# Start addresses of matmul operands moved apart modulo 512 bytes, in a three-block transformer kernel

## The reference

```python
def swiglu(h, w_in, w_out):
    gate, up = jnp.split(h @ w_in, 2, axis=-1)
    return (jax.nn.silu(gate) * up) @ w_out

def first_block(x, ...):
    h = rms_norm(x, ln_pre_mix[l])
    proj = h @ w_in[l]
    ...
    attn_out = dilated_attention(q, k, v).reshape(B, S, ATTN_WIDTH)
    mix = jnp.concatenate([pool_out, attn_out], axis=-1) @ w_out[l]
    x = x + rms_norm(mix, ln_post_mix[l])
    h = rms_norm(x, ln_pre_ffn[l])
    f = (jax.nn.silu(h @ w_gate[l]) * (h @ w_up[l])) @ w_down[l]
    x = x + rms_norm(f, ln_post_ffn[l])

def second_block(x, ...):
    for i in range(DEPTH_2):
        h = rms_norm_2(x, mix_norm[i])
        j = i // N_MIXERS
        if i % N_MIXERS == 0:
            x = x + retention(h, ret_w_in[j], ret_out_norm[j], ret_w_o[j])
        else:
            x = x + stick_breaking(h, sb_w_in[j], sb_q_norm[j], sb_k_norm[j], sb_w_o[j])
        x = x + swiglu(rms_norm_2(x, ffn_norm[i]), ffn_w_in[i], ffn_w_out[i])
```

## The kernel before

| tensor | before | after |
|---|---|---|
| X, HH | 128 | 128 |
| HL | 128 | 160 |
| WH[0], WH[1] | 128, 128 | 224, 288 |
| WL[0], WL[1] | 128, 128 | 128, 160 |
| RAW[0], RAW[1], ACC, ACCH, ACCL | 128 | 160 |
| MEANR, MEAN, IDENT | 0 | 32 |
| MH, M1H, M2H, M3H | 128 | 224 |
| ML | 128 | 32 |
| M1L / M2L / M3L | 128 | 320 / 384 / 448 |
| G1, SG, U1, HD, F (feed-forward work) | 128 | 32 |

## Time and profile before

### The profile page before, as it was taken

One profiled execution on the slowest core, in us unless ns is written; L12 is line 12 of the kernel. 1 busy time (PEld: TensorE's weight loads), 2 busy tenths in 40 slices (PEclk: granted clock), 3 DMA queues, 4 the chain that ended last, 5 costly groups with the idle time before them and its releaser, 6 DMA issues.

```text
span 1964.0 us, 25749 instructions
## 1 busy us (share of the span) xinstructions
PE 1957.2 (100%) x8959; PEld 1590.7 (81%) x8959; DVE 865.8 (44%) x1148; ACT 801.4 (41%) x1078; POOL 764.9 (39%) x307
## 2 busy tenths in 40 slices
PE   9999999999999999999999999999999999999999
PEld 6777888888888778787888888888777788888887
DVE  5775653433145335333243434224788763433200
ACT  6665533233243433324332223225888752323211
POOL 4223344444413334243444444443222244444443
PEclk9999999999999999999999999999999999999999
DMA  5212122223223222222232223222111122222332
GB/s 172 75 65 86 65 97 96 96 96 115 91 74 123 70 86 91 69 87 85 86 105 98 96 96 102 99 99 85 54 63 46 63 97 96 96 96 96 110 97 93
DMA packets 49013, 177.39 MB, mean 90 GB/s; under 512 B 5569, under 2 KB 6465, under 8 KB 48961
## 3 DMA queue, kind: packets, MB, share of 16 engines
q1 hardware_dynamic: 46656, 172.95, 26.3%
q10 hardware_dynamic: 2304, 3.74, 0.6%
HBM read 174.57 MB, written 2.10 MB: 90 GB/s over the span
## 4 chain that ended last, share of the span: by engine, by line
PE 98%; DVE 1%; ACT 0%; DMA 0%; issue 0%; SPq 0%; DVEq 0%; ACTq 0%
PE B L355 26%; PE B L356 26%; PE B L364 26%; PE B L1114 2%; PE B L1251 2%; PE B L1072 1%; PE B L1076 1%; PE B L1073 1%; PE B L381 1%; PE B L377 1%; PE B L376 1%; PE B L1240 1%; PE B L1296 1%; PE B L1158 1%; PE B L900 1%; PE B L931 1%
## 5 line engine op out<-in xcount | busy, mean ns | idle before, releaser
L595 POOL TENSOR_TENSOR WL<-RAW,WH 128x1024 fp32r<-128x1024 f32 (+1 forms) x296 | 753.9, 2549 | 1171.5 <-PE B L364 763.8
L355 PE MATMUL B<-HH,WH 128*128 128x512 f32 x1608 | 629.1, 391 | 0.3 <-DVE QT L2153 0.3
L356 PE MATMUL B<-HL,WH 128*128 128x512 f32 x1608 | 626.1, 389 | 0.0
L336 ACT CAST WH<-RAW 128x1024 fp32r<-128x1024 f32 (+1 forms) x300 | 329.1, 1098 | 555.6 <-PE B L356 475.0
L364 PE MATMUL B<-HH,WL 128*128 128x512 f32 x1608 | 398.3, 390 | 0.0
L355 PEld LDWEIGHTS B<-HH,WH 128*128 128x128 f32 x1608 | 301.8, 188 | 64.9 <-issue 1.7
L364 PEld LDWEIGHTS B<-HH,WL 128*128 128x128 f32 x1608 | 301.4, 188 | 63.2 <-POOL WL L595 0.4
L356 PEld LDWEIGHTS B<-HL,WH 128*128 128x128 f32 x1608 | 301.9, 188 | 62.4
L1921 DVE TENSOR_TENSOR U<-B,RB 128x512 f32<-128x512 f32 x66 | 45.6, 691 | 294.3 <-PE B L364 294.3
L355 PE MATMUL B<-MH,WH 128*128 128x512 f32 x440 | 171.2, 389 | 0.0
L356 PE MATMUL B<-ML,WH 128*128 128x512 f32 x440 | 171.2, 389 | 0.0
(11 more groups left out here) (377 smaller groups left out, 2257.9 us busy)
## 6 DMA issues: line engine op xcount, KB each, us to landing
RAW<-in_w_small SPq DMA_DIRECT2D x254, 512.0 KB, 3.3
RAW<-in_w_large SPq DMA_DIRECT2D x48, 704.0 KB, 4.1
out_t<-X SPq DMA_DIRECT2D x7, 256.0 KB, 5.2
X<-in_x_t ACTq DMA_DIRECT2D x4, 256.0 KB, 6.2
X<-in_x_t SPq DMA_DIRECT2D x4, 256.0 KB, 6.5
DECAY<-in_decay ACTq DMA_DIRECT2D x4, 256.0 KB, 2.6
RAW<-in_w_small ACTq DMA_DIRECT2D x2, 256.0 KB, 6.5
RAW<-in_w_small SPq DMA_DIRECT2D x2, 256.0 KB, 7.4
```

Source lines behind the costliest of these rows:

```text
L336: act.copy(wh, raw).then_inc(s_hi, 1)
L355: pe.matmul(bank, wh[:, c, :], xh[:, k0 + c, :], start=(start and c == 0), stop=False)
L356: mm = pe.matmul(bank, wh[:, c, :], xl[:, k0 + c, :], start=False, stop=False)
L595: pool.tensor_tensor(wl, raw, wh.bitcast(F32), ALU.subtract).then_inc(s_lo, 1)
```

## The change

No instruction is added, removed or moved on any engine, and no DMA: each engine's list of operations, operands, shapes and counts is the same, only source line numbers differ. What changes is where tensors lie. Unused tensors (`PHASE_HL`, `PHASE_WH0`, ...) are allocated ahead of HL, of each WH and WL buffer, of MH and its like (the older `PHASE` grows from 32 to 44 floats), and ahead of ML, M1L, M2L and M3L (`GAP`, `GAP1`, `GAP2`, `GAP3`: 80, 24, 40 and 56 floats). The tensors that are overlaid on these (RAW3, RAW5, RAW6, RAW7, WL3, WL4 and others) are shifted so that they stay over the same tiles.

```diff
--- before.py
+++ after.py
@@ -146,10 +146,16 @@
 
         X = sb("X", [P, DC, T])
         HH = sb("HH", [P, DC, T], F32R)
+        sb("PHASE_HL", [P, 8])
         HL = sb("HL", [P, DC, T], F32R)
         RAW = [sb(f"RAW{s}", [P, HALF, P]) for s in range(2)]
-        WH = [sb(f"WH{s}", [P, HALF, P], F32R) for s in range(2)]
-        WL = [sb(f"WL{s}", [P, HALF, P], F32R) for s in range(2)]
+
+        def weights(name, gap):
+            sb(f"PHASE_{name}", [P, gap])
+            return sb(name, [P, HALF, P], F32R)
+
+        WH = [weights("WH0", 16), weights("WH1", 16)]
+        WL = [weights("WL0", 88), weights("WL1", 4)]
         RB = sb("RB", [P, T])
         ACC = sb("ACC", [P, T])
 
@@ -164,20 +170,21 @@
 
 
 
-        sb("PHASE", [P, 32])
-
-        MH, ML, G1, SG, U1, HD, F = scratch([
-            ("MH", [P, FC, T], F32R), ("ML", [P, FC, T], F32R), ("G1", [P, T]), ("SG", [P, T]),
+        sb("PHASE", [P, 44])
+
+        GAP, GAP1, GAP2, GAP3 = 80, 24, 40, 56
+        MH, _, ML, G1, SG, U1, HD, F = scratch([
+            ("MH", [P, FC, T], F32R), ("PHASE_ML", [P, GAP]), ("ML", [P, FC, T], F32R), ("G1", [P, T]), ("SG", [P, T]),
             ("U1", [P, T]), ("HD", [P, T]), ("F", [P, DC, T])])
 
 
-        _, RAW3, WH3, _, WL3 = scratch([("TILES_H", [P, FC - 4, T]), ("RAW3", [P, DC, P]), ("WH3", [P, DC, P], F32R),
-                                        ("TILES_L", [P, FC - 2, T]), ("WL3", [P, DC, P], F32R)])
-
-        _, RAW7 = scratch([("TILES_M1H", [P, DC * T]), ("RAW7", [P, DC, P])])
-
-        _, RAW5 = scratch([("UP_TO_PR", [P, 26 * T]), ("RAW5", [P, DC, P])])
-        _, RAW6 = scratch([("ALL_TILES", [P, 2 * FC * T]), ("RAW6", [P, HALF, P])])
+        _, RAW3, WH3, _, _, WL3 = scratch([("TILES_H", [P, FC - 4, T]), ("RAW3", [P, DC, P]), ("WH3", [P, DC, P], F32R),
+                                        ("GAP_L", [P, GAP]), ("TILES_L", [P, FC - 2, T]), ("WL3", [P, DC, P], F32R)])
+
+        _, RAW7 = scratch([("TILES_M1H", [P, DC * T + GAP1]), ("RAW7", [P, DC, P])])
+
+        _, RAW5 = scratch([("UP_TO_PR", [P, 26 * T + GAP1]), ("RAW5", [P, DC, P])])
+        _, RAW6 = scratch([("ALL_TILES", [P, 2 * FC * T + GAP]), ("RAW6", [P, HALF, P])])
 
         def tiles_as_weights(x, chunks):
 
@@ -204,9 +211,9 @@
             return BACK.get(u.index, 2) if isinstance(u.m, int) else 2
 
         pad = 16
-        (M1H, M1L, QT1, KT1, VN1, QC, RT, PR, PT, BIAS, CS1, SN1, V1, MX, NM, DEN, RD,
+        (M1H, _, M1L, QT1, KT1, VN1, QC, RT, PR, PT, BIAS, CS1, SN1, V1, MX, NM, DEN, RD,
          UP, WA, WB, INV, DF, YT, WPOOL) = scratch([
-             ("M1H", [P, DC, T], F32R), ("M1L", [P, DC, T], F32R), ("QT1", [P, 2, T]), ("KT1", [P, 2, T]),
+             ("M1H", [P, DC, T], F32R), ("PHASE_M1L", [P, GAP1]), ("M1L", [P, DC, T], F32R), ("QT1", [P, 2, T]), ("KT1", [P, 2, T]),
              ("VN1", [P, 2, TB, P]), ("QC", [P, 2, T]), ("RT", [P, 2, T]), ("PR", [P, 2, WIDE]),
              ("PT", [P, 2, WIDE]), ("BIAS", [P, T]), ("CS1", [P, T]), ("SN1", [P, T]),
              ("V1", [P, T]), ("MX", [P, 2, TB]), ("NM", [P, 2, TB]), ("DEN", [P, 2, TB]), ("RD", [P, 2, TB]),
@@ -214,8 +221,8 @@
              ("INV", [P, POOL_TILES, T]), ("DF", [P, POOL_TILES, T]), ("YT", [P, T]), ("WPOOL", [P, POOL_TILES, P])])
 
 
-        M2H, M2L, CS2, SN2, DECAY, QT2, KT2, SC2, VT2, O2, SG2, TA, TC = scratch([
-            ("M2H", [P, RET_H * RET_VT, T], F32R), ("M2L", [P, RET_H * RET_VT, T], F32R), ("CS2", [P, T]),
+        M2H, _, M2L, CS2, SN2, DECAY, QT2, KT2, SC2, VT2, O2, SG2, TA, TC = scratch([
+            ("M2H", [P, RET_H * RET_VT, T], F32R), ("PHASE_M2L", [P, GAP2]), ("M2L", [P, RET_H * RET_VT, T], F32R), ("CS2", [P, T]),
             ("SN2", [P, T]), ("DECAY", [P, T]), ("QT2", [P, RET_QT, T]), ("KT2", [P, RET_QT, T]), ("SC2", [P, WIDE]),
             ("VT2", [P, TB, T]), ("O2", [P, RET_VT, T]), ("SG2", [P, RET_VT, T]), ("TA", [P, T]), ("TC", [P, T])])
 
@@ -223,8 +230,8 @@
         SQ4, = scratch([("SQ4", [P, DC, T])])
 
         XH_AT = 2 * T + 2 * TB * P + 2 * T + 2 * T + T + 5 * 2 * WIDE + 3 * P
-        (M3H, M3L, QT3, KT3, VN3, QS, SQH, SQL, RQ, ZS, LG, SP, SPH, SPL, LATER, ALL, HEADMEAN, XH, XL) = scratch([
-            ("M3H", [P, DC, T], F32R), ("M3L", [P, DC, T], F32R), ("QT3", [P, 2, T]), ("KT3", [P, 2, T]),
+        (M3H, _, M3L, QT3, KT3, VN3, QS, SQH, SQL, RQ, ZS, LG, SP, SPH, SPL, LATER, ALL, HEADMEAN, XH, XL) = scratch([
+            ("M3H", [P, DC, T], F32R), ("PHASE_M3L", [P, GAP3]), ("M3L", [P, DC, T], F32R), ("QT3", [P, 2, T]), ("KT3", [P, 2, T]),
             ("VN3", [P, 2, TB, P]), ("QS", [P, 2, T]), ("SQH", [P, T], F32R), ("SQL", [P, T], F32R),
             ("RQ", [P, T]), ("ZS", [P, 2, WIDE]),
             ("LG", [P, 2, WIDE]), ("SP", [P, 2, WIDE]), ("SPH", [P, 2, WIDE], F32R), ("SPL", [P, 2, WIDE], F32R),
@@ -233,7 +240,7 @@
 
 
         _, WL4, _, RAW4, _, WH4, _ = scratch([
-            ("TILES_3", [P, 2 * DC, T]), ("WL4", [P, DC, P], F32R), ("UP_TO_XH", [P, XH_AT]),
+            ("TILES_3", [P, 2 * DC * T + GAP3]), ("WL4", [P, DC, P], F32R), ("UP_TO_XH", [P, XH_AT]),
             ("RAW4", [P, DC, P]), ("PAST_RAW4", [P, 2 * P]), ("WH4", [P, DC, P], F32R), ("PAST_WH4", [P, 2 * P])])
         U_LAST = U_OUT3 + 2
 
```

## The result

The changed kernel takes 1998.49 us in the median of 4 runs (1998.36 to 1998.52), against 1965.78 for the kernel before in the same comparison (4 runs, 1965.46 to 1966.02). The ratio is 1.0164, with a 95% interval of 1.0152 to 1.0177. The kernel is slower by 32.7 us.

The account below looks back on a forecast made before the run. TensorE, busy 1957.2 of 1964.0 us, was taken as the bound, at 226.8 ns per matmul. 5.4 ns x 7,700 = 41.6 us on 1965.7 gave 2007 us, range 1940 to 2050 over all cases.

Parts of the forecast that it names:

- the stretch: Feed-forward, 300 to 500 us of the new profile: should hold some 861 matmuls instead of 884.
- Distance 0 is a step of its own: All TensorE matmuls: distance 0 is one at which load and stream fall into a step of 226.8 ns.
- 5.4 ns for each of 7,700 matmuls: High, low, feed-forward output and retention value matmuls: slower by this much each, 41.6 us in sum.
- nine starts behind a MEANR pair: Behind ACCH and ACCL with MEANR (distance 128): nine distance-0 matmuls in 2.09 us, 232.2 ns each.
- The way back: After a disturbance the stream needs some nine matmuls to regain 226.8 ns, slower by 5.4 ns per matmul meanwhile.
- HH and HL alternate, so nothing stays constant for nine matmuls.: High parts with WH: distances 96 and 64, or 160 and 128, alternate; priced like the way back, 5.4 ns each.
- comes back to 227: Timeline sign: a low part of WL[0], at distance 0, returns to 227 ns after its first matmuls.
- 128 bytes is a bad distance: MEANR pair between chunks: at distance 128 its matmuls take 240 ns each, 13 more than the cadence.
- The upper bound: High parts: +13 ns per matmul, each like the MEANR pair; over 7,700 matmuls +100 us.
- much slower: Rival, all 7,700 matmuls: most distances are as bad as 128, +100 us, 2066; over 2040 us counts; chance 0.14.
- The faster rival: Rival, all 7,700 matmuls: some distances are better than 0, giving 1914 or 1943 us; chance 0.24.
- The rule: TensorE's two read ports are independent, so distances cost nothing: 1965.7 us, no change; the prediction argued against it.

Follow-up runs that it names:

- constant runs: Kernel before with weights and tiles moved so each kind of matmul keeps one load-to-stream distance; three in multiples of 32: 2010.08, 1980.54, 2008.36 us; two off-grid: 1997.97, 1995.07 us.

## Why the prediction was right

**The bound and the way.** TensorE's cadence was the only thing that the change could act on, the waits stayed as they were, and so did the other engines' and the transfers' times. All of that held. The forecast was 2007 us, with its own range from 1970 to 2040, and 1998.5 were measured. Of the signs that the prediction named, the groups with HH and HL came to 393 to 396 ns (394 to 396 were forecast), those of MH and ML with WH only to 391 and 390, and the stretch held 865 matmuls where 861 were forecast. "Distance 0 is a step of its own" held for constant distances: of sixteen in multiples of 32 only 256 equals it.

**The size.** 5.4 ns for each of 7,700 matmuls was taken from the nine starts behind a MEANR pair; measured were 32.7 us / 7,700 = 4.2 ns. The direction was right, and the term was too large by a quarter. By the means over the trace, high parts with HH and HL cost 4.6 ns more per matmul than before, their low parts 5.3, high parts with MH and ML 2.2, and their low parts 6.9. Multiplied by 3,216, 1,608, 880 and 429 matmuls that is 28 of the 32.7 us; the rest lies in the smaller groups.

**That the term came so near was luck.** The way back is no price of a distance. It also follows a plain wait in a stream that stays at distance 0. The kernel before, behind the last wait of the earlier trace rows:

```profile
31.72 0.50 PE L355 MATMUL B<-HH,WH 128*128 128x512 f32 x1 [0.25 <-DVE QT L2153]
32.06 0.39 PE L356 MATMUL B<-HL,WH 128*128 128x512 f32 x1
...
33.22 0.39 PE L355 MATMUL B<-HH,WH 128*128 128x512 f32 x1
...
34.12 0.39 PE L355 MATMUL B<-HH,WH 128*128 128x512 f32 x1
```

Five starts in 1.16 us, 232 ns each, and then the next four in 0.90 us, the old step. The 232.2 ns behind the MEANR pair so say what TensorE needs to find its step again after a break, be it a wait or a jump of the distance. A distance that lasts was not in that number; held, most cost 6.0 to 7.8 ns per matmul, and in turn mostly less. The two happen to lie on either side of the 5.4.

**"HH and HL alternate, so nothing stays constant for nine matmuls."** That was the reason for the full price, and it doesn't hold. Alternating distances can be cheaper than a constant one: with the weights moved, letting HL differ from HH by 32 took 6.9 us off. The output projection of the feed-forward shows how much the pairing decides. Two of its units after the change, and ScalarE's first operation on a finished sum:

```profile
499.78 0.39 PE L362 MATMUL B<-MH,WH 128*128 128x512 f32 x1
...
504.78 2.72 PE L371 MATMUL B<-MH,WL 128*128 128x512 f32 x11
507.34 0.39 PE L362 MATMUL B<-MH,WH 128*128 128x512 f32 x1
507.62 0.60 ACT L1399 ACTIVATE SQ<-B 128x512 f32<-128x512 f32 x1 [1.22 <-PE B L371]
...
512.42 2.74 PE L371 MATMUL B<-MH,WL 128*128 128x512 f32 x11
```

An output here is the sum of an even unit and the odd one behind it, so the unit that ends at 507.34 is odd: MH at 64 and ML at 256 in turn. The 22 matmuls of its high part start in 5.00 us, 227.3 ns each, nearly the old step; the low part's 11 (distance 448) take 2.56 us, 232.7 each. The even unit behind it, MH at 0 and ML at 192 in turn, takes 5.08 us for its 22, 230.9 each. (The expectation for HL by 32 has these two the wrong way round.) Held constantly, 64 costs 6.7 ns and 192 costs 2.2; in turn with 0 it is 64 that is nearly free. And 448, held, gave 229. So the cost of a mixture can't be had from the costs of its distances.

**A low part of WL[0] that "comes back to 227".** The prediction named this as something to look for. It happens in half of them: in the unit at 361.63 the last matmuls but one are at 226 to 227 ns, in the unit at 350.49 they are not. With HL alone moved, where every second matmul of the high part ahead is at 0, the step is there from the start. Distance 0 is not enough for the fast step; what stood ahead counts.

**"128 bytes is a bad distance", 240 ns.** Wrong as a price: 128 and 384, held, cost 395 ns, some 233 from start to start, like most others. The 240 of the earlier trace rows belongs to the moment in which the distance jumps from 0 and back: in the changed kernel, with the same distance and no jump from 0, the medians are 389 to 398 ns. That the 240 were caused by the distance at all was right, as the run with MEANR at distance 0 shows.

**The upper bound.** No constant distance came near 240 ns, and the slowest layout tried was 2010 us, so nothing measured here supports the case "much slower", over 2040. **The faster rival** had a chance of 0.24. It fell on all 26 constant distances tried, though not on every combination of them.

**The rule.** By the Trainium skill, "TensorE: Matmul & The Clock Gate", Part 2, the load of the next weights takes nothing from the running matmul's reads. What the prediction drew from it, that distances cost nothing, is not what this case's runs show: where the distance between the two operands is changed and held, a matmul goes from 226.7 to as much as 234 ns. Whether the load then takes from the reads, or something else does, no run shows.

**What stays open.** Why 256 bytes are a period, and why 0, and nearly 192 and 16 ahead, are better than the rest, was not tested: a conflict of the two streams of reads in memory would fit, but no run shows one. Nor is it known why 16 past has two cadences, why even units with the same distances take turns between two, or whether the 13 ns that a matmul has beyond its 512 columns at distance 0 have the same cause. In the constant runs the distance was always that of a load both to its own stream and to the one beside it, and these two were not separated.

## What to carry to other kernels

Where TensorE is busy throughout, compare its start-to-start distance with the columns over the clock, and look for matmuls of the same shape that have another duration: they show what the layout does. Keep loaded and streamed float32r operands at the same address modulo 256 bytes (layouts off it cost 0.7 to 2.3% of this kernel, which is nearly all matmuls), and price such a change per matmul times their number. A short disturbed stretch shows that there is a cost, but not what it will be when the disturbance stays: for that, run the constant case. Before a price is taken from such a stretch, it is worth looking whether the same pattern stands behind an ordinary wait; here it does.

## What the runs showed of the hardware that was not expected

The period is 256 bytes: HL moved by 256 changes nothing (0.9999, 0.9990 to 1.0009), HL moved by 32 costs 15.5 us. A constant distance of 32 to 160 or 224 bytes (or 256 more) costs 6 to 8 ns on each matmul of 512 columns, 192 costs 2, 16 ahead 1 to 2. After a wait in a stream at distance 0 TensorE took five matmuls at 232 ns to come back to its step, after a MEANR pair nine. Distances that alternate have costs of their own: 64 and 256 in turn 227.3 ns, 0 and 192 in turn 230.9. And costs of parts of a layout don't add: 43.8 and 13.8 us for two parts, 32.7 for the whole with a third.
